# Computing the first norm's modulations as they land, and a shorter third mixer

## The chip, the cores and the metric

The program runs on one core of a Trainium2 chip. A core has TensorE (matrix products, here PE), VectorE (DVE), ScalarE (ACT), GpSimd (POOL) and SyncE (SP, which here only issues the loads and stores). The metric is the device time of one execution in microseconds, lower is better. Before the change it is 1545.95 us, the median of three runs (1545.14 to 1545.99).

## The reference

The reference runs three transformer-like layers on 256 tokens of width 1024: two layers of a "first block" and one of a "second block". What touches the change:

```python
def adaln_in(x, g, m, i):                   # norm, then scale and shift made from c
    return rmsnorm(x, g) * (1 + m[:, i, 1][:, None]) + m[:, i, 0][:, None]

cond = jax.nn.silu(c)
for l in range(DEPTH):                      # first block, 2 layers
    m = (cond @ w_mod[l] + b_mod[l]).reshape(bsz, 3, 3, D_MODEL)
    x = x + 0.5 * m[:, 0, 2] * swiglu(adaln_in(x, norm_g[l, 0], m, 0), w1, w3, w2)
    ...                                     # mixer, then a second swiglu
# second block, the third mixer's latent attention (8 heads of 64 + 32)
c_q = rms_norm(proj[..., OFF_CQ:OFF_CKV], q_a_norm)
c_kv = rms_norm(proj[..., OFF_CKV:OFF_KR], kv_a_norm)
q = (c_q @ w_uq).reshape(B_, S_, MLA_HEADS, QK_HEAD)
kv = (c_kv @ w_ukv).reshape(B_, S_, MLA_HEADS, QK_NOPE + V_DIM)
k = jnp.concatenate([k_nope, k_rope_h], axis=-1)   # one rotated part for all heads
q, k = rms_norm(q, q_norm), rms_norm(k, k_norm)    # then the rotary turn of the last 32
```

The very first thing that any layer needs is the shift `m[:, 0, 0]` and the scale `m[:, 0, 1]` of layer 0: 2048 numbers, each a product of `cond` (1024 values) with a column of `w_mod`.

## The kernel before, in words

Activations lie transposed: a chunk is 128 features by 256 tokens, and 8 chunks make the width of 1024. All large products are done in three passes of reduced-precision fp32 (`fp32r`): each weight unit of 128 x 1024 is split by ACT into a high part `WH` (line 1163) and by DVE into a low part `WL` (line 1662), and the activations likewise into `XH`, `XL` (or `GH`, `GL`). PE then sums WH*XH, WH*XL and WL*XH. The feed-forward parts run over 22 hidden chunks c: `up(c)` makes gate and value of chunk c (lines 642, 643, 646), `down(c-1)` adds the chunk before into eight output chunks in PSUM banks 0 to 3 (lines 697, 699, 704). A `low` pass is the one with WL.

The weights come through one SP queue in the order of a list, `stream_plan`, into a ring of three slots; SP waits where a slot is not yet read, and everything behind it in the list waits too. The modulation weights come through the same list, as items of three rows (`mod`, 1.5 MB) into scratch regions; a row is one DVE instruction pair (`mod_row`, line 1719), a 128 x 1024 product with `cond` summed along the free axis. In the prologue six items (18 rows, `HEAD_MODS`) come ahead of all feed-forward weights, DVE reduces them, and only then makes the gain (`adav`), the scaled chunks (line 1698) and their low parts (line 1710). ACT adds the shift (line 1208). The first unit's products, `first_up` (lines 658 and 664), take the chunks as they come.

In the third mixer (`win2_and_attention`) the twelve projection units of `win2` (line 781) are interleaved by hand with the latent attention's own products, which are in plain fp32: `q_pair` (lines 1002, and 1004 for the 32 swapped columns that the rotary turn needs), `lru_products` (line 1068), `k_pair` (lines 1015, and 1016, which copies the rotated key part `kr` through PE), `values` (1022), the sums of squares `cq_stats` (1031) and `q_stats` (1038), `k_sums` (1047, 1048) and `k_spread` (1058). A plain fp32 product is two passes in the trace. ACT's `gates` (line 1473) start when the low part of the memory's norm is done (`norm_low`, "mem", line 1708 on DVE); DVE also turns the queries (`q_rope`, lines 2160, 2161, 2167) and runs the short convolutions (`lru_convs`, line 2148). `take(b, ...)` makes PE wait for the last reader of bank b.

At the end of the last feed-forward part, the low pass of chunk 20 (line 681) is interleaved with the twenty-first's three passes (line 686).

Of the kernel before, what the change touches and what calls it, by code (L numbers as in the profile page):

```python
# [26 lines left out]
HEAD_MODS = 6  # L27
# [12 lines left out]
def columns(spec):  # L40
# [14 lines left out]
    ("eps", 1), ("inv", 1), ("halfpi", 1)])  # L55
# [9 lines left out]
def mod_plan():  # L65


    slot = {i: i for i in range(HEAD_MODS)}
    slot.update({i: i % 4 for i in range(HEAD_MODS, 20)})
# [4 lines left out]
    for f, (a, b, late) in enumerate([(HEAD_MODS, 20, 1), (22, 34, 1), (34, 46, 0), (46, 48, 2)]):  # L74
        n = b - a
        ffns[f] = {(k * (NFF - 1)) // n: a + k for k in range(n)}
        for c, i in ffns[f].items():
            for r in range(MOD_ROWS):
                h = 2 * c + late + r
                rows.setdefault((f, h // 2, h % 2), []).append((i, r))  # L80
# [10 lines left out]
def stream_plan():  # L91
# [3 lines left out]
    items = [(("mod", i), ITEM) for i in range(HEAD_MODS)]  # L95
# [42 lines left out]
WEIGHTS = [name for name, _ in ITEMS if name[0] not in ("mod", "lru")]  # L138
# [50 lines left out]
def build(nc, stream, param_d, const_d, bias_d, filter_d, x_d, mem_d, pos_d, c_d, out_d, known):  # L189
# [44 lines left out]
    def halves(name):  # L234
# [4 lines left out]
                 ring[:, (RING - 1) * ITEM:RING * ITEM]]  # L239
    rel = scr[:, ITEM:2 * ITEM].rearrange("p (h m) -> p h m", m=384)  # L240
# [31 lines left out]
    def landed(name):  # L272
# [3 lines left out]
        if name[0] == "mod":  # L276
            k = MOD_SLOT[name[1]]
            return sig.sem(f"mod_landed{k}"), 16 * sum(MOD_SLOT[i] == k for i in range(name[1] + 1))
# [45 lines left out]
    in_done = {8 * (3 * l + i) + 5: (l, i) for l in range(2) for i in range(3)}  # L324
# [202 lines left out]
    with nc.Block() as block:  # L527
# [3 lines left out]
        def _(sp):  # L531
            sp.dma_start(par[:, :], param_d).then_inc(*mark("par_in", n=16))
            sp.dma_start(cond[:, :], c_d.partition_broadcast(P)).then_inc(*mark("c_in", n=16))
            sp.dma_start(con[:, 0:2 * P], const_d[:, 0:2 * P]).then_inc(*mark("ones_in", n=16))
            for name, n in ITEMS:
                if name[0] == "mod":
                    i = name[1]
                    k = MOD_SLOT[i]
                    for p in [p for p in range(i) if MOD_SLOT[p] == k][-1:]:
                        sp.wait_ge(*at("mod_read", p))  # L540
# [11 lines left out]
                else:  # L552
                    i = PLACE[name]
                    if i == RING - 1:
                        sp.wait_ge(*at("mod_read", HEAD_MODS - 1))
# [7 lines left out]
                if name == ("mod", 1):  # L563
                    sp.dma_start(X, x_d).then_inc(*mark("x_in", n=16))
                if name == ("ffn", 0, 2):
                    sp.wait_ge(*at("mod_read", 4))
# [24 lines left out]
        def _(pe):  # L591
# [37 lines left out]
            def ffn(f):  # L629
# [19 lines left out]
                def first_up(b):  # L649

                    units = list(enumerate(up_units(f, 0)))
                    for k in range(KD):
                        pe.wait_ge(*at("norm_high", key, k))
                        for a, u in units:
                            for which, w in ((WH, ("high", u)), (WL, low_of(u))):
                                if k == 0:
                                    pe.wait_ge(*at(*w))
                                pe.matmul(b[:, a * S:(a + 1) * S], part(which, u, k), XH[:, k, :],  # L658
                                          start=(which is WH and a == 0 and k == 0), stop=False, skip_group_check=True)
                    for a, u in units:  # L660
# [5 lines left out]
                        last.then_inc(*mark("w1_used" if a == 0 else "ffn_up", f, 0))  # L666

                def down(c):
# [6 lines left out]

                    if c == NFF - 1:
# [23 lines left out]
                    if c == NFF - 2:  # L700
                        return
# [278 lines left out]
            uq = m[:, 0:1536].rearrange("p (k h n) -> p k h n", k=2, h=8)  # L980
            uq_swapped = m[:, 1536:2048].rearrange("p (k h n) -> p k h n", k=2, h=8)
# [11 lines left out]
            def q_pair(p):  # L993
                take(4 + p % 2, "q_turned", p)
                take(6 + p % 2, "q_turned", p)
# [3 lines left out]
                for i in range(2):  # L999
                    cols = slice(i * S, (i + 1) * S)  # L1000
                    for k in range(2):
                        pe.matmul(bank[4 + p % 2][0:96, cols], uq[:, k, 2 * p + i, :], PR[:, 8 + k, body], start=(k == 0), stop=(k == 1))
                    for k in range(2):
                        last = pe.matmul(bank[6 + p % 2][64:96, cols], uq_swapped[:, k, 2 * p + i, :], PR[:, 8 + k, body],
                                         start=(k == 0), stop=(k == 1))
                last.then_inc(*mark("q_product", p))

            def k_pair(p):
                take(4 + p % 2, "k_copied", p)
                if p == 0:  # L1010
                    pe.wait_ge(*at("normed", "ckv", 0))
                    pe.wait_ge(*at("kr_turned"))
                for i in range(2):
                    cols = slice(i * S, (i + 1) * S)
                    pe.matmul(bank[4 + p % 2][0:64, cols], uk[:, 2 * p + i, :], lat[:, 2, :], start=True, stop=True)
# [3 lines left out]
            def values():  # L1019
                for t in range(2):  # L1020
                    take(6 + t, "v_copied", t)
                    pe.matmul(bank[6 + t], lat[:, 2, t * P:(t + 1) * P], uv, start=True, stop=True)\
                        .then_inc(*mark("v_product", t))
# [9 lines left out]
            def q_stats():  # L1033

                pe.wait_ge(*at("q_squared", 3))
                for t in range(2):
                    for h in range(8):
                        last = pe.matmul(bank[6][:, 8 * t + h:8 * t + h + 1], SQ[0:96, h, t * P:(t + 1) * P], ones[0:96, 0:1],
                                         start=True, stop=True)
                last.then_inc(*mark("q_stat"))  # L1040
# [45 lines left out]
            def win2_and_attention():  # L1086
# [20 lines left out]
                cq_stats()  # L1107
                k_sums()
                q_stats()
# [42 lines left out]
        def _(act):  # L1152
# [295 lines left out]
            act.wait_ge(*at("c_in"))  # L1448
            act.activation(cond[:, :], cond[:, :], ACT.Silu).then_inc(*mark("cond"))
            for l in range(2):  # L1450
                if l == 0:
                    norm(("sub", 0, 0), lambda c: [("x_in",)], ahead=up_units(0, 0)[1])
# [1004 lines left out]
```

## Time and profile before

| | |
|---|---|
| median of three runs | 1545.95 us |
| the profiled execution | 1537.43 us |
| its span, first to last instruction | 1535.3 us |
| around the span | 2.1 us |
| PE busy | 1439.9 us, 94% |
| DVE busy | 1124.1 us, 73% |
| ACT busy | 705.1 us, 46% |
| DMA traffic | 309.29 MB |

Busy shares are means over the whole span, so the first 50 us and single stretches of the third mixer must be read by themselves. "Idle before" is the time an engine stood still ahead of an instruction, with the one that ended it. The granted clock is that of TensorE: 1.00 is 2.4 GHz, 0.50 is 1.2 GHz.

### The profile page before, as it was taken

What the parts mean: (1) busy time and instruction counts of PE and PEld (TensorE: products, weight loads), DVE (VectorE), ACT (ScalarE), POOL (GpSimd) and SP (SyncE); (2) the same over time, 40 slices, a digit from 0 to 9 for tenths busy, and PEclk for the clock granted to TensorE, in tenths of its full rate; (3) what the DMA queues carried; (4) which work ended last, traced back from release to release, by engine and by line L of the source; (5) the groups of instructions that cost most, each with busy time, mean ns of one, the idle gap of its engine ahead of it and who ended that gap; (6) DMA issues with size and microseconds to landing.
All of it is one profiled execution on the core that took longest, in us unless ns stands there. A gap on an engine that the chain in (4) does not pass through costs nothing.

```text
span 1535.3 us, 26554 instructions
## 1 busy us (share of the span) xinstructions
PE 1439.9 (94%) x10992; PEld 1349.6 (88%) x10992; DVE 1124.1 (73%) x1849; ACT 705.1 (46%) x1126; POOL 19.3 (1%) x16
## 2 busy tenths in 40 slices
PE   1999999999999989999999999999999879899998
PEld 1999998788999989999898689999976759799998
DVE  6888988867777788887667766565692766677776
ACT  2434445444343453334445344343544855554543
POOL 0000000000000000010000000000000120000000
PEclk8999999999999999999999999999999979999999
DMA  9986865156777548657333146654312203344541
GB/s 391 415 351 249 339 244 221 55 202 249 283 296 283 224 199 329 283 210 325 143 137 111 34 162 231 230 210 179 130 77 96 110 15 136 125 165 176 196 175 73
DMA packets 32327, 309.29 MB, mean 201 GB/s; under 512 B 3496, under 2 KB 5800, under 8 KB 7504
## 3 DMA queue, kind: packets, MB, share of 16 engines
q1 hardware_dynamic: 32208, 307.60, 52.0%
q8 instruction: 87, 1.43, 0.4%
q14 instruction: 32, 0.26, 0.0%
HBM read 306.53 MB, written 1.06 MB: 200 GB/s over the span
## 4 chain that ended last, share of the span: by engine, by line
PE 83%; DVE 10%; issue 3%; ACT 2%; DMA 2%; SPq 0%; DVEq 0%; ACTq 0%
PE bank L642 13%; PE bank L646 13%; PE bank L643 13%; PE bank L781 12%; PE bank L697 6%; PE bank L699 6%; PE bank L704 6%; DVE WL L1662 2%; PE bank L612 2%; PE bank L658 2%; DMA PR<-in_stream 1%; PE bank L861 1%; PE bank L686 1%; PE bank L850 1%; DVE tmp L1680 1%
## 5 line engine op out<-in xcount | busy, mean ns | idle before, releaser
L1662 DVE TENSOR_TENSOR WL<-ring,WH 128x1024 fp32r<-128x1024 f32 x420 | 504.1, 1226 | 51.3 <-ACT WH L1163 49.1
L1163 ACT ACTIVATE WH<-ring 128x1024 fp32r<-128x1024 f32 x420 | 429.6, 1053 | 135.2 <-PE bank L781 52.6
L642 PE MATMUL bank<-XH,WH 128*128 128x256 f32 x1680 | 410.1, 283 | 1.4 <-ACT WH L1163 1.4
L643 PE MATMUL bank<-XL,WH 128*128 128x256 f32 x1680 | 407.8, 281 | 0.0
L642 PEld LDWEIGHTS bank<-XH,WH 128*128 128x128 f32 x1680 | 316.2, 188 | 7.6 <-issue 6.0
L643 PEld LDWEIGHTS bank<-XL,WH 128*128 128x128 f32 x1680 | 316.2, 188 | 1.0 <-issue 1.0
L646 PE MATMUL bank<-XH,WL 128*128 128x256 f32 x1680 | 233.8, 282 | 1.0 <-DVE WL L1662 1.0
L646 PEld LDWEIGHTS bank<-XH,WL 128*128 128x128 f32 x1680 | 214.0, 188 | 1.2 <-DVE WL L1662 1.2
L1237 ACT ACTIVATE SG<-bank 128x256 f32<-128x256 f32 x88 | 33.8, 384 | 377.0 <-PE bank L646 363.5
L697 PE MATMUL bank<-GH,WH 128*128 128x256 f32 x840 | 202.6, 279 | 0.7 <-ACT WH L1163 0.7
L699 PE MATMUL bank<-GL,WH 128*128 128x256 f32 x840 | 202.5, 279 | 0.0
L697 PEld LDWEIGHTS bank<-GH,WH 128*128 128x128 f32 x840 | 157.5, 188 | 0.9 <-ACT WH L1163 0.9
L699 PEld LDWEIGHTS bank<-GL,WH 128*128 128x128 f32 x840 | 157.6, 188 | 0.0
L1784 DVE TENSOR_TENSOR tmp<-SG,bank 128x256 f32<-128x256 f32 x88 | 37.0, 421 | 154.6 <-ACT SG L1237 147.4
L704 PE MATMUL bank<-GH,WL 128*128 128x256 f32 x800 | 110.3, 279 | 0.0
L704 PEld LDWEIGHTS bank<-GH,WL 128*128 128x128 f32 x800 | 101.2, 188 | 0.0
L781 PE MATMUL bank<-XH,WH 128*128 128x256 f32 x512 | 90.4, 302 | 10.6 <-ACT XH L1208 7.1
L781 PEld LDWEIGHTS bank<-XH,WH 128*128 128x128 f32 x512 | 75.3, 199 | 21.6 <-issue 17.9
L781 PE MATMUL bank<-XH,WL 128*128 128x256 f32 x512 | 82.5, 285 | 0.0
L1771 DVE SCALAR_TENSOR_TENSOR scr<-bank,par,scr 128x255 f32<-128x255 f32 x88 | 38.4, 478 | 49.0 <-ACT scr L1230 48.2
L781 PE MATMUL bank<-XL,WH 128*128 128x256 f32 x512 | 74.1, 288 | 0.0
L781 PEld LDWEIGHTS bank<-XH,WL 128*128 128x128 f32 x512 | 72.4, 192 | 0.0
(306 smaller groups left out, 1698.8 us busy)
## 6 DMA issues: line engine op xcount, KB each, us to landing
ring<-in_stream SPq DMA_DIRECT2D x133, 1536.0 KB, 6.6
scr<-in_stream SPq DMA_DIRECT2D x15, 1536.0 KB, 10.8
PR<-in_stream SPq DMA_DIRECT2D x15, 1536.0 KB, 8.3
att<-in_stream SPq DMA_DIRECT2D x15, 1536.0 KB, 10.1
ring<-in_stream SPq DMA_DIRECT2D x8, 1024.0 KB, 5.0
ring<-in_stream SPq DMA_DIRECT2D x11, 512.0 KB, 3.6
kf_mix<-in_stream SPq DMA_DIRECT2D x2, 1536.0 KB, 16.0
con<-in_consts SPq DMA_DIRECT2D x1, 2000.0 KB, 19.7
```

The source lines that it names most:

```text
L642: pe.matmul(o, part(WH, u, k), XH[:, k, :], start=(k == 0), stop=False)
L643: pe.matmul(o, part(WH, u, k), XL[:, k, :], start=False, stop=False)
L646: last = pe.matmul(o, part(WL, u, k), XH[:, k, :], start=False, stop=(k == KD - 1))
L697: pe.matmul(out(m), part(WH, u, m), GH[:, c % 2, :], start=(c == 0 and m % 2 == 0), stop=False, skip_group_check=True)
L699: pe.matmul(out(m), part(WH, u, m), GL[:, c % 2, :], start=False, stop=False, skip_group_check=True)
L704: last = pe.matmul(out(m), part(WL, u, m), GH[:, c % 2, :], start=False, stop=False, skip_group_check=True)
L781: last = pe.matmul(o, lhs, rhs, start=first, stop=(p == parts[-1] and k == kc - 1), skip_group_check=True)
L1163: act.activation(part_all(WH, u), raw(u), ACT.Copy).then_inc(*mark("high", u))
L1237: act.activation(SG[:, c % 2, :], guc[:, c % 2, 0, :] if f == 4 else bank[4 + c % 2][:, 0:S], ACT.Silu)\
L1662: dve.tensor_tensor(part_all(WL, u), raw(u), part_all(WH, u).bitcast(F32), ALU.subtract)\
L1771: ins = dve.scalar_tensor_tensor(o, src, prm("fconv_w", 2 * NFF * k + col), o, ALU.mult, ALU.add)
L1784: dve.tensor_tensor(G32, SG[:, c % 2, :], second, ALU.mult).then_inc(*mark("g32", f, c))
```

## The change

There are three parts.

First, the prologue. The first 16 of the modulation's columns of layer 0 (8 of shift, 8 of scale) come as eight `head` items of 1 MB, one for each chunk: the scale's row for DVE and the shift's 1024 x 128 weights for PE. DVE reduces eight scale rows instead of 18 rows; PE makes each shift as eight plain fp32 products with one moving column (`cond_col`); ACT copies it out with its bias. Item 5 of the modulations (now the first `mod`) goes into a region that heads 1 and 2 use, so SP waits for both to be read. `first_up` has shifts and the low parts woven in for the first feed-forward.

Second, the last feed-forward's chunk 20 does its low pass itself, ahead of chunk 21.

Third, the mixer: the swapped query columns join the plain ones (96 + 32 = 128 columns in one product), the key's rotated part is copied by POOL instead of PE, `q_stats` goes pair by pair behind `k_pair`, `values` and `cq_stats` move.

```diff
-HEAD_MODS = 6
+HEAD_MODS = 5
     def ffn(f):
         for c in range(NFF + 1):
+            if (f, c) == (0, 0):
+                items.extend((("head", k), 2 * D) for k in range(3))
+            if (f, c) == (0, 1):
+                items.extend((("head", k), 2 * D) for k in range(3, KD))
...
+    head_before = {0: 1, 1: 2, 2: 4, 3: 5, 4: 7}
+                    if before:
+                        sp.wait_ge(*at("mod_read", before[-1]))
+                    else:
+                        sp.wait_ge(*at("scale_row", head_before[k]))
+                        sp.wait_ge(*at("shift_sum", head_before[k]))
...
                     for k in range(KD):
+                        if f == 0:
+                            for c in {0: range(4)}.get(k, range(k + 1, k + 2) if 3 <= k < 7 else ()):
+                                shift(c)
                         pe.wait_ge(*at("norm_high", key, k))
...
+                        if f == 0 and k >= 2:
+                            lows(k - 2)
...
+                def shift(c):
+                    pe.wait_ge(*at(f"head_landed{c}"))
...
+                    for k in range(KD):
+                        last = pe.matmul(bank[SHIFT_BANK[c]][:, c:c + 1], w[:, k, :], cond_col[:, k:k + 1], start=(k == 0), stop=(k == KD - 1),
+                                         skip_group_check=True)
+                    last.then_inc(*mark("shift_sum", c))
...
+                    if c == NFF - 1 and f == 4:
+                        pe.wait_ge(*at(*low_of(u)))
+                        for m in range(KD):
+                            for w, x in ((WH, GH), (WH, GL), (WL, GH)):
...
-                    for k in range(2):
-                        pe.matmul(bank[4 + p % 2][0:96, cols], uq[:, k, 2 * p + i, :], PR[:, 8 + k, body], start=(k == 0), stop=(k == 1))
-                    for k in range(2):
-                        last = pe.matmul(bank[6 + p % 2][64:96, cols], uq_swapped[:, k, 2 * p + i, :], PR[:, 8 + k, body],
-                                         start=(k == 0), stop=(k == 1))
+                    for k in range(2):
+                        last = pe.matmul(bank[4 + p % 2][:, cols], uq[:, k, 2 * p + i, :], PR[:, 8 + k, body], start=(k == 0),
+                                         stop=(k == 1))
...
-                    last = pe.matmul(bank[4 + p % 2][64:96, cols], ident[64:96, 64:96], kr, start=True, stop=True)
...
+                values(0)
+                cq_stats()
                 for p in range(4):
                     k_pair(p)
-                values()
+                    q_stats(p)
+                values(1)
...
+                    pool.wait_ge(*at("kr_turned"))
+                    for h in range(8):
+                        if h == 6:
+                            pool.wait_ge(*at("q_product", 3))
+                        ins = pool.tensor_copy(k96_pairs[h // 2][64:96, h % 2, :], kr)
...
+            for c in range(3):
+                scale_row(c)
+            norm_root(first)
+            for c in range(3):
+                head_scaled(c)
+            split_to(up_units(0, 0)[1])
+            for c in range(3, KD):
+                scale_row(c)
+                head_scaled(c)
+                norm_lows(first, range(c - 3, c - 2))
+            norm_lows(first, range(KD - 3, KD))
```

The SP queue at the program's start, before (the six `mod` items ahead of the first weights in `ring`):

```order
L534 DMA con<-in_consts 128x256
L548 DMA scr<-in_stream 128x3072 x2
L564 DMA X<-in_x 128x2048
L548 DMA PR<-in_stream 128x3072
L548 DMA att<-in_stream 128x3072
L548 DMA kf_mix<-in_stream 128x3072
L548 DMA ring<-in_stream 128x3072
L559 DMA ring<-in_stream 128x2048
L548 DMA PR<-in_stream 128x3072 [waits mod_read]
L559 DMA ring<-in_stream 128x3072
```

and after (128x2048 into `scr`, `PR`, `att` and `kf_mix` are heads 0 to 7):

```order
L544 DMA con<-in_consts 128x256
L545 DMA X<-in_x 128x2048
L548 DMA scr<-in_stream 128x2048 x3
L574 DMA ring<-in_stream 128x2048
L565 DMA scr<-in_stream 128x3072 [waits shift_sum,scale_row]
L548 DMA PR<-in_stream 128x2048 x2
L548 DMA att<-in_stream 128x2048
L548 DMA kf_mix<-in_stream 128x2048 x2
L574 DMA ring<-in_stream 128x3072
L565 DMA PR<-in_stream 128x3072 [waits shift_sum,scale_row]
```

Heads 3 to 7 now stand behind a wait for PE's and DVE's work on head 2.

PE from the norm's sums on, after (`knorm` holds `cond_col`; L708 is a shift's product, L684 the high and low-weight passes of `first_up`, L670 its low-activation passes). Before, nothing stands between the sums and the first `XH` products:

```order
L626 MATMUL bank<-SQ,con 128x256 [waits squared] x7
L708 MATMUL bank<-knorm,scr 128x1 [waits cond_col,head_landed0]
L708 MATMUL bank<-knorm,scr 128x1 x7
L708 MATMUL bank<-knorm,scr 128x1 [waits head_landed1]
L708 MATMUL bank<-knorm,scr 128x1 x7
L708 MATMUL bank<-knorm,scr 128x1 [waits head_landed2]
L708 MATMUL bank<-knorm,scr 128x1 x7
L708 MATMUL bank<-knorm,PR 128x1 [waits head_landed3]
L708 MATMUL bank<-knorm,PR 128x1 x7
L684 MATMUL bank<-XH,WH 128x256 [waits high,norm_high]
L684 MATMUL bank<-XH,WL 128x256 [waits low_dve]
```

Four shifts stand ahead of the first product with the norm's result, and one more is woven in ahead of each of chunks 3 to 6.

PE in the third mixer behind `lru_products`, before:

```order
L1015 MATMUL bank<-kf_mix,ring 64x256 [waits k_copied]
L1016 MATMUL bank<-tmp,con 32x256
L1015 MATMUL bank<-kf_mix,ring 64x256
L1016 MATMUL bank<-tmp,con 32x256
L1022 MATMUL bank<-ring,kf_mix 128x512 [waits q_turned] x2
```

and after (L1069 is `values`, L1077 `cq_stats`, L1062 `k_pair`, L1084 `q_stats`):

```order
L1069 MATMUL bank<-ring,kf_mix 128x512 [waits normed,kr_turned]
L1077 MATMUL bank<-con,kf_mix 128x1 [waits cq_squared,stat_root]
L1077 MATMUL bank<-con,kf_mix 128x1 x3
L1062 MATMUL bank<-kf_mix,ring 64x256 [waits normed,q_turned]
L1062 MATMUL bank<-kf_mix,ring 64x256
L1084 MATMUL bank<-con,SQ 128x1 [waits q_squared]
L1084 MATMUL bank<-con,SQ 128x1 x3
```

The copies through PE are gone, and the one-column sums of the queries stand between the key products.

## Rows read from the trace of the kernel before

**Rows 1.** The page's chain that ended last, share of the span by engine.
```profile
PE 83%; DVE 10%; issue 3%; ACT 2%; DMA 2%; SPq 0%; DVEq 0%; ACTq 0%
```
**Rows 2.** Timeline of 0 to 50 us: start, duration (us), engine, line, operation, idle before.
```profile
10.88 1.28 DVE L1719 CUSTOM_DVE_ANT_0 scr<-scr,cond,par 128x1024 f32<-128x1024 f32 x1 [10.88 <-DMA scr<-in_stream]
16.82 2.56 ACT L1187 ACTIVATE SQ<-X 128x256 f32<-128x256 f32 x8 [8.29 <-DMA X<-in_x]
17.38 5.48 PE L612 MATMUL bank<-SQ,con 128*128 128x256 f32 x16 [17.38 <-ACT SQ L1187]
...
33.97 2.00 ACT L1163 ACTIVATE WH<-ring 128x1024 fp32r<-128x1024 f32 x2 [10.53 <-DMA ring<-in_stream]
40.29 0.58 PE L658 MATMUL bank<-XH,WH 128*128 128x256 f32 x1 [17.42 <-ACT XH L1208]
46.24 2.06 PE L664 MATMUL bank<-XL,WH 128*128 128x256 f32 x16
49.72 0.39 PE L642 MATMUL bank<-XH,WH 128*128 128x256 f32 x1 [1.42 <-ACT WH L1163]
```
**Rows 3.** The page's DMA issues: form, count, KB each, us from issue to landing.
```profile
ring<-in_stream SPq DMA_DIRECT2D x133, 1536.0 KB, 6.6
ring<-in_stream SPq DMA_DIRECT2D x8, 1024.0 KB, 5.0
```
**Rows 4.** Stretches of the prologue: busy us (instructions) by engine, granted clock, DMA share, GB/s.
```profile
28.00:29.00 1.00, 0.00 (x0) 0.00 (x0) 1.00 (x3) 0.00 (x0) 0.00 (x0) 0.50 0.95 406
45.00:46.00 1.00, 1.00 (x10) 1.00 (x10) 0.63 (x2) 0.00 (x0) 0.00 (x0) 1.00 0.98 418
```
**Rows 5.** PE's groups by line, 1120 to 1195 us: busy us, mean ns.
```profile
L1004 PE MATMUL bank<-PR,ring 128*32 128x256 f32 x32 | 8.4, 384 | 0.0
```
**Rows 6.** Stretches of half a microsecond around the one-column sums, same columns as rows 4.
```profile
1181.00:1181.50 0.50, 0.50 (x6) 0.50 (x7) 0.50 (x1) 0.00 (x0) 0.00 (x0) 1.00 1.03 442
1182.00:1182.50 0.50, 0.50 (x4) 0.50 (x3) 0.24 (x1) 0.00 (x0) 0.00 (x0) 0.50 0.93 393
1188.50:1189.00 0.50, 0.50 (x6) 0.50 (x6) 0.00 (x0) 0.00 (x0) 0.00 (x0) 1.00 0.00 0
```
**Rows 7.** The chain that ended last, 1155 to 1194 us: start, us, what.
```profile
1155.34 0.48 ACT scr L1473
1155.86 5.45 PE bank L1068 x24
...
1169.15 0.57 PE bank L1015 x2
1169.72 0.55 PE bank L1016 x2
...
1179.89 5.38 PE bank L1038 x32
1185.27 4.40 PE bank L781 x24
```
**Rows 8.** Stretches of the mixer, same columns as rows 4.
```profile
1127.00:1140.00 13.00, 12.55 (x70) 8.05 (x69) 12.70 (x22) 6.06 (x12) 0.00 (x0) 1.00 0.01 2
1140.00:1152.40 12.40, 12.40 (x71) 8.02 (x70) 11.91 (x28) 1.37 (x3) 0.00 (x0) 1.00 0.00 0
```
**Rows 9.** POOL's and DVE's timelines near 1223 us.
```profile
1223.63 2.46 POOL L1631 TENSOR_TENSOR scr<-scr 128x1024 f32<-128x1024 f32 x1 [536.81 <-ACT scr L1562]
1243.39 0.72 POOL L1637 TENSOR_TENSOR PR<-PR,scr 128x256 f32<-128x256 f32 x1
...
1223.79 3.38 DVE L1662 TENSOR_TENSOR WL<-ring,WH 128x1024 fp32r<-128x1024 f32 x1
```
**Rows 10.** Timeline of the program's end, PE.
```profile
1526.49 0.55 PE L681 MATMUL bank<-GH,WL 128*128 128x256 f32 x1 [2.47 <-issue]
1529.62 0.33 PE L686 MATMUL bank<-GL,WH 128*128 128x256 f32 x1
1531.67 0.28 PE L686 MATMUL bank<-GH,WL 128*128 128x256 f32 x1
```

More of the change, by code:

```diff
@@ L65, in mod_plan @@
 def mod_plan():
-    slot = {i: i for i in range(HEAD_MODS)}
-    slot.update({i: i % 4 for i in range(HEAD_MODS, 20)})
+    slot = {i: i % 4 for i in range(HEAD_MODS, 20)}
     slot.update({20: 0, 21: 4})
@@ L91, in stream_plan @@
 def stream_plan():
-    items = [(("mod", i), ITEM) for i in range(HEAD_MODS)]
+    items = []
     units = []
@@ L137 @@
 ITEMS, UNITS = stream_plan()
-WEIGHTS = [name for name, _ in ITEMS if name[0] not in ("mod", "lru")]
+WEIGHTS = [name for name, _ in ITEMS if name[0] not in ("head", "mod", "lru")]
 PLACE = {name: i for i, name in enumerate(WEIGHTS)}
@@ L277, in landed @@
             k = MOD_SLOT[name[1]]
-            return sig.sem(f"mod_landed{k}"), 16 * sum(MOD_SLOT[i] == k for i in range(name[1] + 1))
+            return sig.sem(f"mod_landed{k}"), 16 * sum(MOD_SLOT[i] == k for i in range(HEAD_MODS, name[1] + 1))
         i = PLACE[name]
@@ L674, in out @@
                         return bank[m // 2][:, (m % 2) * S:(m % 2 + 1) * S]
+                    if c == NFF - 1 and f == 4:
+                        pe.wait_ge(*at(*low_of(u)))
+                        for m in range(KD):
+                            for w, x in ((WH, GH), (WH, GL), (WL, GH)):
+                                last = pe.matmul(out(m), part(w, u, m), x[:, c % 2, :], start=False, stop=(w is WL),
+                                                 skip_group_check=True)
+                            last.then_inc(*mark("ffn_out", f, m))
+                        return
                     if c == NFF - 1:
@@ L1448, in _, with shift, high @@
             act.wait_ge(*at("c_in"))
+            act.activation(cond_col[:, :], prm("c_col", 0, KD), ACT.Silu).then_inc(*mark("cond_col"))
             act.activation(cond[:, :], cond[:, :], ACT.Silu).then_inc(*mark("cond"))
+            def shift(c):
+                act.wait_ge(*at("shift_sum", c))
+                act.activation(modv[:, c:c + 1], bank[SHIFT_BANK[c]][:, c:c + 1], ACT.Identity, bias=prm("b_mod", c)).then_inc(*mark("shift", c))
+            def high(c):
+                act.wait_ge(*at("shift", c))
+                act.wait_ge(*at("scaled", ("sub", 0, 0), c))
+                act.activation(XH[:, c, :], norm_sq(("sub", 0, 0), c), ACT.Identity, bias=modv[:, c:c + 1])\
+                    .then_inc(*mark("norm_high", ("sub", 0, 0), c))
             for l in range(2):
                 if l == 0:
-                    norm(("sub", 0, 0), lambda c: [("x_in",)], ahead=up_units(0, 0)[1])
+                    squares(("sub", 0, 0), lambda c: [("x_in",)])
+                    load_table(ACT.Sqrt)
+                    root(("sub", 0, 0))
+                    for c in range(4):
+                        shift(c)
+                        if c == 2:
+                            split_to(up_units(0, 0)[1])
+                    for c in range(KD):
+                        if c >= 4:
+                            shift(c)
+                        high(c)
                 else:
@@ L2389, in lay_out @@
             blocks["mod", MOD_ITEMS * l + k] = m[k]
+    w = f["w_mod"][0]
+    shift = w[:, :D].reshape(KD, P, KD, P).transpose(2, 1, 0, 3)
+    scale = w[:, D:2 * D].T.reshape(KD, P, D)
+    for k in range(KD):
+        blocks["head", k] = np.concatenate([scale[k], shift[k].reshape(P, D)], 1)
     def ffn(n, w1, w3, w2):
```

123 lines of the change are left out of this document (74 added, 49 removed).

## Prediction

> **What bounds the kernel now.** The chain that ended last comes first: 83% of the span is PE [rows 1], so what takes PE's time, or makes it wait, is what counts. Three places are changed, and each must be read by itself, because the mean over the span says nothing of them.
>
> The prologue: the timeline shows PE idle for 17.42 us before its first product of the norm at 40.29, and the first unit ends at 48.30 (46.24 + 2.06); the second starts at 49.72 [rows 2]. Ahead of that stands DVE with its 18 rows of modulation, from 10.88 on [rows 2]. The loads keep the DMA engines full (share 0.95 to 0.98) [rows 4], so bytes count too. Two landings give their rate: the first item (2.4 MB with all ahead of it) is there at 10.88, the first weights (11.9 MB) at 33.97 [rows 2], which makes 2.43 us for each MB.
>
> The mixer: the chain runs over ACT's first gate at 1155.34, then without a gap over PE [rows 7]. But in the 25 us ahead of it DVE is busy for 12.70 of 13.00 and 11.91 of 12.40 us [rows 8]: both engines are full there.
>
> The end: PE stands still for 2.47 us before 1526.49, then has 32 products of which the last starts at 1531.67 [rows 10].
>
> **Prologue, step by step.** DVE loses ten rows ahead of the first unit; PE gains 8 shifts of 8 products of one column, each two passes: 128 passes. Their form is that of the one-column sums: 32 passes in 5.38 us [rows 7], of which about 1.86 us at the granted clock 1.00 (6 to 7 begun or running in each half microsecond) and 3.52 us at 0.50 (4) [rows 6]. This is 0.12 us each at 2.4 GHz (15.5 of them) and 0.21 at 1.2 GHz (16.5): 1.9 or 3.4 us for a shift.
>
> Which clock? PE was busy 0.50 of 0.50 us with these sums when the clock fell to 0.50, and it came back at 1188.5, about 3.3 us after the 256-column products had begun at 1185.27 [rows 6, 7]. The Trainium skill (TensorE: Matmul & The Clock Gate, What's actually happening) says that the gate is set by how busy PE has been recently. Read by the busy share, this would keep the clock up through the shifts; the row disagrees, since PE was fully busy and fell. I take the row: one-column passes don't hold the clock. What the other reading makes is the first rival.
>
> The times. x is now behind only 0.9 MB: 9.7 us (10.88 less 0.5 MB). Squares and sums take 6.0 us (16.82 to 22.86) [rows 2]: 15.7. Shifts 0 to 2 then need 5.7 us at 2.4 GHz, 10.2 at 1.2; I take 7.3, the clock falling on the way: 23. SP waits for shift 2 before it issues modulation item 5 (1.5 MB) and heads 3 to 7; the 5.9 MB ahead of them had landed by 19.4, so DMA stands empty. A load alone takes 5.0 us for 1 MB and 6.6 for 1.5 [rows 3], so about 2 us are fixed; head 3 lands at 23 + 2.1 + 2.5 x 2.43 = 31.2, head 7 at 40.9.
>
> PE has been idle for 8 us then, longer than the 5.1 us after which the clock was 0.50 in before (22.86 to 28) [rows 2, 4]. Shift 3 at 1.2 GHz ends at 34.6; ACT's copy and first high part take 0.7 (35.3). A 256-column pass costs 0.21 to 0.22 at this clock (14 from 1526.49 to 1529.62) [rows 10] and 0.12 at 2.4 GHz [rows 2]. Chunks 0 to 2 and the low part of 0 are 14 passes, 3.0 us: 38.3. Then four times a shift, four high and two low passes, 3.4 + 1.3 = 4.7 us: 57.0. Ten passes close it: 59.1. The 3.0 us of wide products should bring the clock back once, for some 3 us in which twice the work is done: 56. Before it was 48.3: +7.7. ACT's silu and split behind it stay (1.42 us [rows 2]); the second unit may start at 1.2 GHz where before it was at 1.00 [rows 4], +0.3. Sum +8.0. Bounds: +13.8 if all of it, shifts 0 to 2 too, is at 1.2 GHz (26.0, 34.2, 62.1), -3.8 if nothing is (shift 2 at 21.5, head 3 at 29.7, end 44.5). DVE needs 2.4 us for each late chunk and is hidden behind PE's 4.7; if PE took 2.6, it would be the two side by side. Two more rows of modulation fall to DVE inside the first feed-forward, where PE waited for DVE nowhere: 0.
>
> **Mixer, step by step.** Removed on PE: 32 passes of swapped columns. They show as 8.4 us busy in the row, overlapped; at 0.245 each they are 7.8 us of wall time [rows 5]. But DVE is as full as PE in that stretch [rows 8], and nothing is taken from DVE; ACT's gates wait for DVE's last low part of the memory's norm, at 1155.34 [rows 7]. So these 7.8 us bring 0: PE will wait for DVE's turned queries and ahead of the gates instead. It then waits for over 5 us, and starts the 24 passes of line 1068 at 1.2 GHz, +1.7 (half of some 3.4 us).
>
> From there PE is the chain. The key copies go, 8 times 0.55 [rows 7]: -4.4. The 32 one-column passes now stand in pairs between key products, at 0.12: 3.8 instead of 5.38, -1.6; unit 11 behind them took 4.40 for 24 passes, 2.84 at full clock, -1.6. `k_spread` needs the root of `k_sums`, 0.5 on ACT and 1.7 on DVE; unit 11 covers it with 2.84. Sum -5.9 with +1.7 in it.
>
> Added on POOL: eight copies of 32 x 256, beside DVE's full stretch. No such copy is in the trace; the nearest is a two-input operation of 128 x 256, 0.72 us undisturbed [rows 9]. When POOL's 2.46 us operation began at 1223.63, DVE's split, begun at 1223.79, took 3.38 us in place of some 1.2: it stood until POOL was done [rows 9]. Bounds: 0 and 8 x 0.72 = 5.8; some fall beside DVE's reciprocal or its PSUM readers, so I take 2.3. Mixer: -3.6, between -7.6 (no cold start, no lock) and -0.1 (both, the lock at 5.8). The Trainium skill (SBUF — State Buffer, Who interferes with whom) calls the port pair of the two an exclusive lock, where the second fully blocks if DVE reads two SBUF operands. DVE's convolutions and splits do; by it the sum would be nearer to the upper bound, which is the second rival.
>
> **End.** Eight of the 32 passes move into the 2.47 us of waiting. The other 24 take 2.8 us at 2.4 GHz instead of 5.35 (-2.5), or 4.3 if the clock still falls (15 at 0.21) (-1.1) [rows 10]. The idle time shrinks to 1.5 us; I take -2.2.
>
> **Sum.** +8.0 - 3.6 - 2.2 = +2.2. The profiled execution took 1537.43 us, 1535.3 of span and 2.1 around it: 1539.6. It was 8.5 us (0.55%) below the median of the runs shown, 1545.95; the difference is carried over as it is: 1548.2 us. About 0.2%, 3.1 us, is what a measurement of this kernel can tell from no change.
>
> **Rivals.**
> 1. The one-column passes do hold or restore the clock. For: before 17.38 PE had been idle, and nothing in the page says what counts; against: rows 6. Then shifts 0 to 2 end at 21.5, head 3 lands at 29.7, shift 3 is still slow (33.1), and all behind it fast: 14 x 0.12 = 1.7, four times 2.6, 1.2: 47.2 with ACT's 0.7, -1.1. Total -1.1 - 3.6 - 2.2 = -6.9: 1539.0. Chance 0.16.
> 2. POOL's lock: slower. Each of the eight copies holds DVE's two-operand work for its full 0.72 us; +5.8 in place of 2.3 makes the mixer -0.1, the total +5.7: 1551.7. For: rows 9; against: 32 partitions and one input may be shorter. From a DVE delay of 3.2 us on, the sum is over the 3.1 us. Chance 0.15.
> 3. The clock stays at 1.2 GHz through the whole of the first unit, without the one recovery: 59.1, or up to 62.1. +11 to +14 in place of 8: about 1552 to 1554. Chance 0.12.
> 4. PE is the bound in the mixer after all, and DVE follows: -7.8 - 4.4 - 3.2 = -15.4; total -9.6: 1536.3. Against: rows 8. Chance 0.06.
> The forecast has 0.51, with a range of its own of 1545 to 1551.
>
> **Chances.** Faster than by 0.2%: rival 1, rival 4 and 0.03 of the forecast's case, 0.25. Slower: rivals 2 and 3 and a fifth of the forecast's case, 0.37. Within: 0.38. The range leaves out rival 4 and the far end of 3: 1538.5 to 1554.
>
> **What would show it.** Right: SP's issue of the `mod` item behind the first weights waits for PE until 21 to 25 us; DMA has an empty stretch near 20 to 25; the clock is 0.50 through most of 31 to 56, with the shifts' passes at 0.21 us; the second unit begins at 56 to 60. In the mixer PE idles ahead of the third `q_pair` and over 5 us ahead of the gates, which begin at the same distance from the stretch's start as before or later; POOL's copies stand beside lengthened DVE operations; 8 passes fill the wait at the end. Wrong: the second unit begins before 50 us, or the gates begin over 3 us earlier.

## The result, and the profile after

| | before | after |
|---|---|---|
| median of 20 runs each | 1545.97 us (1540.26 to 1550.83) | 1553.75 us (1541.32 to 1557.39) |
| ratio | | 1.0046, 95% interval 1.0029 to 1.0062 |
| profiled execution, span | 1537.43, 1535.3 us | 1554.27, 1552.5 us |
| mean granted clock | 0.979 | 0.963 |

The change makes the kernel some 7 us slower. The median is inside the forecast's range by 0.25 us, and not where the forecast put it: the prologue loses more than was said, and that is nearly all of the difference.

**Prologue.** The timeline after (start, duration, engine, line, operation, idle before), to set beside [rows 2]; L708 is a shift's product, L656 the second unit:

```profile
9.59 6.50 PE L626 MATMUL bank<-SQ,con 128*128 128x256 f32 x16 [9.59 <-ACT SQ L1235]
15.93 7.71 PE L708 MATMUL bank<-knorm,scr 128*128 128x1 f32 x48
...
23.73 0.33 SPq L565 DMA_DIRECT2D scr<-in_stream  x1
...
32.59 3.57 PE L708 MATMUL bank<-knorm,PR 128*128 128x1 f32 x16 [8.96 <-DMA PR<-in_stream]
40.07 3.41 PE L708 MATMUL bank<-knorm,PR 128*128 128x1 f32 x16
44.76 3.41 PE L708 MATMUL bank<-knorm,att 128*128 128x1 f32 x16
...
62.69 0.55 PE L656 MATMUL bank<-XH,WH 128*128 128x256 f32 x1 [1.51 <-ACT WH L1211]
```

Stretches of it (busy us by engine in the order PE, PEld, DVE, ACT, POOL, then granted clock, DMA share, GB/s), to set beside [rows 4]:

```profile
16.00:17.00 1.00, 1.00 (x12) 1.00 (x10) 0.67 (x1) 0.47 (x1) 0.00 (x0) 1.00 1.04 442
18.00:19.00 1.00, 1.00 (x9) 1.00 (x10) 1.00 (x1) 0.07 (x1) 0.00 (x0) 0.85 0.02 8
22.00:23.00 1.00, 1.00 (x6) 1.00 (x6) 0.00 (x0) 0.00 (x0) 0.00 (x0) 0.50 0.00 0
50.00:51.00 1.00, 1.00 (x6) 1.00 (x6) 0.00 (x0) 0.00 (x0) 0.00 (x0) 0.50 0.92 393
60.00:61.00 1.00, 1.00 (x6) 0.88 (x5) 0.00 (x0) 0.00 (x0) 0.00 (x0) 0.50 1.07 455
66.00:67.00 1.00, 1.00 (x9) 1.00 (x8) 1.00 (x2) 0.00 (x0) 0.00 (x0) 0.76 0.93 400
```

SP issues the waiting item at 23.73, 0.1 us after the last product of shift 2, and DMA moves next to nothing at 18 and nothing at 22 us. PE then has nothing for 8.96 us. The clock falls to 1.2 GHz near 19 us, while PE is busy 1.00 of 1.00 us with one-column passes, and is back only in the microsecond that begins at 66. The second unit starts 13.0 us later than at 49.72 [rows 2].

**Mixer.** PE's timeline after (L1052 `q_pair`, L1115 the gates' products, L1062 `k_pair`, L1084 `q_stats`, L902 the first scores), to set beside [rows 7]:

```profile
1163.21 3.78 PE L1052 MATMUL bank<-PR,ring 128*128 128x256 f32 x8 [4.36 <-DVE kf_mix L2257]
...
1178.42 7.13 PE L1115 MATMUL bank<-scr,att 128*128 128x256 f32 x24 [4.20 <-ACT scr L1543]
...
1187.13 1.08 PE L1062 MATMUL bank<-kf_mix,ring 128*64 128x256 f32 x4
1188.14 1.05 PE L1084 MATMUL bank<-con,SQ 96*128 96x1 f32 x8
...
1209.66 2.68 PE L902 MATMUL bank<-PR,kf_mix 96*128 96x256 f32 x6
```

The 7.8 us that the merge takes from PE are idle time now: 4.36 us ahead of the third pair, and 4.20 us ahead of the gates' products where 1.51 us stood before. Behind the gates, key products and sums in pairs take about 1.0 us each.

POOL's copies and DVE at the same time (`WL` is a split with two SBUF inputs, `kf_mix` a scaling):

```profile
1150.18 3.16 POOL L1703 COPY PR<-tmp 32x256 f32<-32x256 f32 x6 [444.37 <-DVE tmp L2235]
1172.56 0.74 POOL L1703 COPY PR<-tmp 32x256 f32<-32x256 f32 x2 [19.21 <-PE bank L1052]
...
1150.15 1.22 DVE L1740 TENSOR_TENSOR WL<-ring,WH 128x1024 fp32r<-128x1024 f32 x1
1153.07 0.55 DVE L1776 SCALAR_TENSOR_TENSOR kf_mix<-PR,par,tmp 128x256 f32<-128x256 f32 x1
```

and the same scaling before:

```profile
1130.62 0.48 DVE L1698 SCALAR_TENSOR_TENSOR kf_mix<-PR,par,tmp 128x256 f32<-128x256 f32 x1
```

DVE's split takes 1.22 us, the page's mean for this line (1225 ns). The scaling began under the sixth copy and took 0.07 us longer than before; no other DVE operation there is lengthened. The eight copies by themselves (least, median and longest, ns):

```profile
L1703 POOL COPY PR<-tmp x8: 393/395/1448, 1150.2 to 1172.9; 32x256 f32<-32x256 f32 x8
```

**End.** PE's timeline, to set beside [rows 10]:

```profile
1542.69 1.12 PE L756 MATMUL bank<-GH,WL 128*128 128x256 f32 x8
1545.26 0.36 PE L724 MATMUL bank<-GH,WH 128*128 128x256 f32 x1 [1.46 <-issue]
1548.09 0.28 PE L724 MATMUL bank<-GH,WL 128*128 128x256 f32 x1
```

From the first to the last start are 2.83 us for 24 passes, where it was 5.18 for 32.

### The profile page after: what moved, and what is told of

The parts are those of the page before. It is cut to its first block, busy times and chain, and to the rows that moved or that the text cites. A ratio compares the mean times of both kernels' runs of the same rounds, so it can differ in the third digit from the quotient of the medians.

```text
span 1552.5 us, 26743 instructions
## 1 busy us (share of the span) xinstructions
PE 1466.1 (94%) x11072; PEld 1385.9 (89%) x11072; DVE 1116.7 (72%) x1840; ACT 707.6 (46%) x1135; POOL 23.2 (1%) x24
## 4 chain that ended last, share of the span: by engine, by line
PE 85%; DVE 9%; issue 3%; ACT 2%; DMA 1%; SPq 0%; DVEq 0%; ACTq 0%
PE bank L656 13%; PE bank L660 13%; PE bank L657 13%; PE bank L833 12%; PE bank L749 6%; PE bank L751 6%; PE bank L756 6%; PE bank L626 2%; PE bank L684 2%; DVE WL L1740 2%; PE bank L708 2%; PE bank L913 1%; PE bank L902 1%; PE bank L738 1%; DVE tmp L1758 1%
## 5 line engine op out<-in xcount | busy, mean ns | idle before, releaser
L1740 DVE TENSOR_TENSOR WL<-ring,WH 128x1024 fp32r<-128x1024 f32 x420 | 503.9, 1225 | 54.4 <-ACT WH L1211 50.4
L656 PE MATMUL bank<-XH,WH 128*128 128x256 f32 x1680 | 411.0, 283 | 1.5 <-ACT WH L1211 1.5
L656 PEld LDWEIGHTS bank<-XH,WH 128*128 128x128 f32 x1680 | 317.8, 189 | 7.8 <-issue 7.8
L749 PE MATMUL bank<-GH,WH 128*128 128x256 f32 x840 | 206.2, 284 | 0.8 <-ACT WH L1211 0.8
L751 PE MATMUL bank<-GL,WH 128*128 128x256 f32 x840 | 206.2, 281 | 0.0
L1849 DVE SCALAR_TENSOR_TENSOR scr<-bank,par,scr 128x255 f32<-128x255 f32 x88 | 38.5, 478 | 50.1 <-ACT scr L1278 49.3
```

Source lines behind the costliest of these rows:

```text
L656: pe.matmul(o, part(WH, u, k), XH[:, k, :], start=(k == 0), stop=False)
L749: pe.matmul(out(m), part(WH, u, m), GH[:, c % 2, :], start=(c == 0 and m % 2 == 0), stop=False, skip_group_check=True)
L751: pe.matmul(out(m), part(WH, u, m), GL[:, c % 2, :], start=False, stop=False, skip_group_check=True)
L1740: dve.tensor_tensor(part_all(WL, u), raw(u), part_all(WH, u).bitcast(F32), ALU.subtract)\
L1849: ins = dve.scalar_tensor_tensor(o, src, prm("fconv_w", 2 * NFF * k + col), o, ALU.mult, ALU.add)
```

## The experiments

The ratios are to runs of the kernel before on the same chip; its medians beside e1 to e4, e5 to e8 and e9 to e12 were 1544.21, 1542.66 and 1543.13 us.

**The parts apart.** e1 has the diff's hunks of the prologue, e2 those of the mixer and the end.

> Only the first part of the change (heads, shifts on PE, scale rows on DVE), the mixer and the end as before. Theory A (the loss is made in the prologue, by a late second unit): the second unit starts 10 to 14 us later than in the kernel before and the whole is 9 to 16 us slower, ratio 1.006 to 1.010. Rival B (the whole change's loss is mostly falls of the granted clock at other places, which one profile of each shows by chance): the prologue alone costs under 5 us. Forecast on record: +8.0.

> The mixer's and the end's parts alone, the prologue as before. Theory A: 6 to 8 us faster (mixer -4 to -6, end -2.3), ratio 0.995 to 0.996. Rival B (the mixer brings nothing, since a cold start of the scores behind it and of the gates' products takes the gain): -2 to -3, ratio 0.998 to 0.999. POOL's eight copies beside DVE: by the rows of the changed kernel 0, by the lock of the prediction +2 to +6, which would show as gates' products that begin later against the stretch's start.

Measured: e1 1558.7 us, ratio 1.0092 (1.0061 to 1.0123), +14.2 us. e2 1538.3 us, 0.9958 (0.9936 to 0.998), -6.5 us. The sum, +7.7, is close to the whole change's +7.1. All of the loss is in the prologue; rival B of e1 falls (the lower end of e1's interval is +9.4 us), and the -2 to -3 us of e2's rival lie just outside e2's interval (-3.1 to -9.9).

**The queue and the width.** e3 lets no load wait for shift 2:

```diff
 def ffn(f):                                # stream_plan
-            if (f, c) == (0, 1):
-                items.extend((("head", k), 2 * D) for k in range(3, KD))
...
             items.append((("ffn", f, c), UNIT * len(names)))
+            if (f, c) == (0, 0):
+                items.extend((("head", k), 2 * D) for k in range(3, KD))
             if c in MODS_OF.get(f, {}):
```

> As the first, with one edit: heads 3 to 7 stand in the load queue ahead of the modulation item that waits for shift 2, so no load waits for PE. Theory A: head 3 lands at 21 instead of 32.6 us, PE goes from shift 2 to shift 3 without a gap, first unit ends near 52 instead of 61, whole 8 to 10 us faster than the first kernel (ratio to before 1.000 to 1.003). Rival C (the eight shifts at 1.2 GHz are what takes the time, the empty queue is covered): the first unit ends at 57 or later, under 4 us faster than the first.

The first unit then ends at 50.1 us, which excludes rival C's 57 or later.

e9 changes only the width of a shift's moving operand, e5 both:

```diff
-    cond_col = knorm
+    cond_col = sb("cond_wide", P + 8)       # silu of 136 columns, the last 8 are c's
...
-   pe.matmul(bank[SHIFT_BANK[c]][:, c:c + 1], w[:, k, :], cond_col[:, k:k + 1], ...
+   pe.matmul(bank[SHIFT_BANK[c]][:, 0:P], w[:, k, :], cond_col[:, k + 1:k + 1 + P], ...
```

> As e3_order, and the moving operand of a shift's products is 128 columns wide instead of one (the 128th column is the wanted one, the others are read and left in PSUM). Theory A (one-column passes let the clock fall and don't bring it back, wide ones hold it): granted clock 1.00 from 15 us on, a shift in 1.9 to 2.2 instead of 3.4 us, chunk period 2.6 instead of 4.7, first unit ends at 38 to 41 instead of 50.1, ratio to before 0.995 to 0.998. Rival E (the clock falls because of something else that these products share, their plain fp32 form or the small gaps between them): clock 0.50 from about 20 us on, and the wider passes make it slower than e3_order, ratio 1.003 or over.

> As e1_prologue, with only the 128 column wide moving operand; heads 3 to 7 still behind the item that waits. Theory A (two causes, the queue's wait and the clock, that can be taken away one by one): shifts 0 to 2 end at 20 to 21 instead of 23.8, head 3 lands 2.5 to 3.5 us earlier, at 29 to 30; PE has been idle for 9 us and the clock is 0.50 when it starts again, but the wide passes bring it back some 5 us later; the second unit starts at 49 to 54 instead of 62.6; ratio to before 0.999 to 1.004, between e1 and e5. If the clock were the only cause: as e5, 0.996.

| | one column | 128 columns |
|---|---|---|
| heads 3 to 7 behind the wait | e1: 1.0092, +14.2 us, unit 2 at 62.55 | e9: 1.0037 (1.0022 to 1.0052), +5.7 us, unit 2 at 50.90 |
| ahead of it | e3: 1.0027 (1.0008 to 1.0045), +4.2 us, unit 2 at 51.61 | e5: 0.9961 (0.9939 to 0.9983), -6.0 us, unit 2 at 41.39 |

The timeline of e3:

```profile
21.52 3.57 PE L708 MATMUL bank<-knorm,PR 128*128 128x1 f32 x16 [0.89 <-DMA PR<-in_stream]
28.99 3.41 PE L708 MATMUL bank<-knorm,PR 128*128 128x1 f32 x16
...
51.61 0.36 PE L656 MATMUL bank<-XH,WH 128*128 128x256 f32 x1 [1.51 <-ACT WH L1207]
```

PE's idle time ahead of shift 3 is 0.89 instead of 8.96 us. And of e5:

```profile
29.06 1.95 PE L708 MATMUL bank<-cond_wide,att 128*128 128x128 f32 x16
31.56 1.95 PE L708 MATMUL bank<-cond_wide,kf_mix 128*128 128x128 f32 x16
...
37.48 0.87 PE L670 MATMUL bank<-XL,WH 128*128 128x256 f32 x6
...
41.39 0.55 PE L656 MATMUL bank<-XH,WH 128*128 128x256 f32 x1 [3.04 <-ACT WH L1207]
```

A shift of 128 columns takes 1.95 us, one of a single column 3.41. The same microsecond in e3 and in e5:

```profile
30.00:31.00 1.00, 1.00 (x7) 1.00 (x6) 0.93 (x5) 0.00 (x0) 0.00 (x0) 0.50 1.06 442
```

```profile
30.00:31.00 1.00, 1.00 (x11) 1.00 (x11) 1.00 (x3) 0.00 (x0) 0.00 (x0) 1.00 1.10 459
```

PE is busy 1.00 us in both; one is at 1.2 GHz, the other at 2.4. Only the moving operand's width differs between the two kernels, so the width is the cause. Theory A's numbers for the first unit came in (its end: 38.4), and so did the ratio. The clock did not stay up for good: it fell in PE's idle time of 3.04 us ahead of the second unit and read 0.50 from 40 to 46 us. Rival E (the plain fp32 form or the gaps) falls. The Trainium skill (TensorE: Matmul & The Clock Gate, What's actually happening) says that the gate is set by how busy the PE has been recently. By the busy time that the profile shows, this would have kept e3 at full clock; the measurement decides, and the sentence holds here only if "busy" means something else than that share.

In e9 the queue's wait stands:

```profile
29.67 3.78 PE L708 MATMUL bank<-cond_wide,PR 128*128 128x128 f32 x16 [8.74 <-DMA PR<-in_stream]
...
37.35 2.19 PE L708 MATMUL bank<-cond_wide,PR 128*128 128x128 f32 x16
40.10 1.95 PE L708 MATMUL bank<-cond_wide,att 128*128 128x128 f32 x16
```

Shift 3 is slow behind 8.74 us of idle time, wide or not (3.78); the clock is back in the microsecond from 37, about 8 us after PE had started again, where some 5 were expected. In e1, with one column, it is back only in the microsecond from 65. Head 3 lands at 29.7 and the second unit starts at 50.90, both as expected. So the order alone is worth 10.0 us, the width alone 8.5, both 20.2. By the intervals each of these differences is known to some 5 us; by the start of unit 2 they are 10.9, 11.7 and 21.2. There are two causes, nearly additive.

**Another way to the same end.** e4 is e3 with the shifts of chunks 4 to 7 as rows on DVE:

```diff
+                if c >= PE_SHIFTS:          # 4
+                    s = head_slots[c][:, D:2 * D]
+                    dve.tensor_tensor_reduce(s, s, cond[:, :], 1.0, prm("b_mod", c), ALU.mult, ALU.add,
+                                             accum_out=modv[:, c:c + 1]).then_inc(*mark("shift", c))
```

> As the third, and shifts 4 to 7 are made by DVE as rows, like the scales (1.3 us each), and only 0 to 3 by PE. Theory A (3.4 us on PE for a shift of one-column passes at 1.2 GHz is the dear part once the queue is free): PE has shifts 0 to 3 behind it at 27, DVE ends its rows near 42, first unit ends at 43 to 46, second unit 3 to 6 us earlier than in the kernel before; ratio 0.996 to 0.999. Rival D (DVE becomes the bound, since it was full in the prologue of the kernel before): first unit ends at 48 or later, ratio 1.000 or over.

Measured: 1544.09 us, 1.0002 (0.998 to 1.0024). The first unit ends at 46.0, the late edge of what was expected; the second starts at 47.45, 2.3 us earlier than before instead of 3 to 6, and the runs don't tell that from nothing. DVE is the bound in it: PE waits for DVE's low parts four times, 1.04 to 2.43 us each.

```profile
36.30 0.79 PE L674 MATMUL bank<-XL,WH 128*128 128x256 f32 x2 [2.43 <-DVE XL L1783]
```

So rival D's mechanism takes most of the gain. e4 also shows when the clock comes back without one-column passes: behind shift 3 it has only wide ones, 18 of them from 27.65 to about 31.9 us, and the clock is at 1.00 in the microsecond from 33. It is at 0.50 again in that from 36, behind the wait of 2.43 us (columns as in the stretches above):

```profile
33.00:34.00 1.00, 0.87 (x6) 0.67 (x6) 1.00 (x3) 0.05 (x1) 0.00 (x0) 1.00 1.01 430
36.00:37.00 1.00, 0.70 (x3) 0.70 (x4) 1.00 (x2) 0.45 (x1) 0.00 (x0) 0.50 0.98 418
```

**The mixer's parts.** e7 is the kernel before with the merge of the query columns alone, e6 is e2 without it (the merge is the diff's lines of `q_pair`, with the matching ones of `q_rope`).

> The kernel before with only the merge of the swapped query columns into the plain ones. Theory A: PE's 7.8 us turn into idle time ahead of the third pair and of the gates, 0 to +2 us, ratio 1.000 to 1.001. Rival F: -4 to -8 us, ratio 0.995 to 0.997.

> As e2_mixer_tail, but the swapped query columns are products of their own again, as in the kernel before (32 more passes). Theory A (DVE sets the pace there, the merge only makes PE idle and lets its clock fall ahead of the gates): the gates' products begin at the same place against the stretch's start, take 5.5 instead of 7.1 us, whole 0 to 2 us faster than e2 (ratio to before 0.994 to 0.996). Rival F (PE is the bound, the merge is worth its passes): 4 to 8 us slower than e2, ratio 0.999 to 1.001.

Measured: e7 1547.18 us, 1.0014 (0.9992 to 1.0035); e6 1538.07 us, 0.9949 (0.9924 to 0.9974) beside e2's 0.9958. Neither shows a gain or a loss of the merge beyond its interval; rival F's 4 to 8 us are excluded. The place shows why. From the memory norm's last sums to the gates' products are 36.15 us before (1119.71 to 1155.86), 36.09 after (1142.33 to 1178.42), 35.78 in e7, 36.05 in e6, 35.71 in e2: PE's work between does not set it. e7:

```profile
1148.56 3.53 PE L1000 MATMUL bank<-PR,ring 128*128 128x256 f32 x8 [3.95 <-DVE kf_mix L2157]
...
1163.78 8.18 PE L1064 MATMUL bank<-scr,att 128*128 128x256 f32 x24 [5.25 <-ACT scr L1469]
```

What the merge takes from PE comes back as 3.95 and 5.25 us of idle time, and the gates' products take 8.18 instead of 5.45 us. In e6 they took 7.13 behind only 1.92 us of idle time, so the start at 1.2 GHz that e6 should have saved was there without the merge too; that half of my expectation missed. In the six other profiles without the merge (before, e1, e3, e4, e5, e9) the wait is 1.51 to 1.63 us and the products take 5.45. So the 1.7 us are not shown to be the merge's alone.

e12 is e2 with the key's rotated part copied by PE again:

```diff
-                    last = pe.matmul(bank[4 + p % 2][0:64, cols], uk[:, 2 * p + i, :], lat[:, 2, :], start=True, stop=True)
+                    pe.matmul(bank[4 + p % 2][0:64, cols], uk[:, 2 * p + i, :], lat[:, 2, :], start=True, stop=True)
+                    last = pe.matmul(bank[4 + p % 2][64:96, cols], ident[64:96, 64:96], kr, start=True, stop=True)
```

> As e2_mixer_tail, but the rotated key part is copied by PE again, eight products of 0.55 us between the key products, instead of by POOL. Theory A: scores begin 4 to 4.6 us later against the memory norm's sum than in e2 (66.9), at about 71.3; ratio to before 0.998 to 0.999. If POOL's copies had cost DVE something (the lock), the difference is smaller, down to 0.

Measured: 1548.22 us, 1.0038 (1.0018 to 1.0058), some 12 us over e2 by the ratios. I had expected 4 to 5: a miss, and by much. From the gates' products to the scores are 47.94 us (1157.12 to 1205.06) against 31.21 in e2. The timeline of e12 (L1019 key products, L1020 the copies, L1042 the sums):

```profile
1168.46 0.61 PE L1020 MATMUL bank<-tmp,con 32*32 32x256 f32 x2
1169.00 1.64 PE L1042 MATMUL bank<-con,SQ 96*128 96x1 f32 x8
1170.58 1.11 PE L1019 MATMUL bank<-kf_mix,ring 128*64 128x256 f32 x2
1171.62 1.06 PE L1020 MATMUL bank<-tmp,con 32*32 32x256 f32 x2
...
1186.36 1.87 PE L1042 MATMUL bank<-con,SQ 96*128 96x1 f32 x8
```

At 1169 the clock falls, and stays at 0.50 until the full-width products of unit 10; between, copies of 32 x 32 weights and one-column sums alternate, and each takes twice its time. In the kernel before, copies and key products alternate without such sums from 1161.24 to 1170.20, each copy at 0.55 us. The sums in pairs kept the clock up only without the copies, and not always then. The same stretch is 31.17 to 31.40 us long in four profiles of the new mixer (after, e2, e6, e10), and 34.42 and 34.46 in two (e8, e11), where the clock fell in it. In e11:

```profile
1166.00:1169.00 3.00, 3.00 (x18) 2.17 (x18) 0.00 (x0) 2.60 (x6) 0.00 (x0) 0.92 0.00 0
1169.00:1172.00 3.00, 3.00 (x12) 2.14 (x11) 0.00 (x0) 1.57 (x4) 0.00 (x0) 0.50 0.00 0
```

With the old mixer it was 37.36 in the profile of before and 38.92 to 39.25 in five others (e1, e3, e4, e5, e9), so the typical gain here is 1.6 us larger than before's own profile says. At the end it is the other way round: the old end's 32 passes took 5.18 us in before's profile and 5.11 in e7's, where the clock was at 0.50 for some of them, but 3.78 or 3.79 in those five, at full clock (in e3 from 1540.23 to 1544.02). Against 2.83 that is 1.0 us instead of 2.35.

**Put together.** e8 is the changed kernel with e4's prologue, e10 with e5's two edits, e11 moves one item more:

```diff
-            if c in MODS_OF.get(f, {}):
+            if (f, c) == (0, 1):
+                items.append((("mod", MODS_OF[0][0]), ITEM))
+            if c in MODS_OF.get(f, {}) and (f, c) != (0, 0):
                 items.append((("mod", MODS_OF[f][c]), ITEM))
```

> The changed kernel with e4_half's prologue (heads 3 to 7 ahead of the waiting item, shifts 4 to 7 on DVE). Theory A (the parts add up): before + e4 (0) + e2 (-6.5): ratio 0.995 to 0.997, and 13 to 15 us under the changed kernel. If the parts don't add (the clock's falls move and eat the gain): 0.998 or over.

> The changed kernel with e5's two edits (heads 3 to 7 ahead of the waiting item, moving operand of 128 columns). If the parts add up: e5 (-4.5 to -6) and e2 (-6.5): 11 to 13 us under before, ratio 0.991 to 0.993.

> As e10, and the first modulation item of 1.5 MB stands behind the second unit's weights instead of ahead of them. Theory: in e5 PE stood idle 3.04 us ahead of the second unit for these weights and fell to 1.2 GHz there (41.4 to 47); now they land 3.6 us earlier, the wait is ACT's split alone (about 1.5), the clock stays at 1.00: second unit starts at 39.9, another 2 to 4 us less than e10, ratio 0.989 to 0.991. Rival: the wait was not the loads' but ACT's and DVE's; no change to e10.

Measured: e8 1537.65 us, 0.9965 (0.9942 to 0.9988); e10 1530.43 us, 0.9922 (0.9899 to 0.9944); e11 1529.71 us, 0.9914 (0.9893 to 0.9935). The parts add up within the intervals in all three; e8 is by the ratios 12.5 us under the changed kernel, where 13 to 15 were expected. e10 is 12.0 us under the kernel before, and by ratios (1.0046 against 0.9922) some 19 us under the changed kernel. The difference between e10 and e11 is not resolved, so the further 2 to 4 us are a miss, and their mechanism is not seen either: e10's second unit starts at 40.85, e11's at 40.99, both behind ACT's split.

```profile
40.85 0.36 PE L656 MATMUL bank<-XH,WH 128*128 128x256 f32 x1 [1.63 <-ACT WH L1211]
```

```profile
40.99 0.36 PE L658 MATMUL bank<-XH,WH 128*128 128x256 f32 x1 [1.51 <-ACT WH L1213]
```

PE's wait ahead of the second unit, 3.04 us in e5, is 1.63 in e10, so there was hardly anything for e11 to take. In e5 ACT had waited 1.42 us for these weights until 40.19; in e10 it began its split at 39.65 without a wait. Why e10's weights were there in time and e5's not stays open.

## Why the prediction was right in its range and wrong in its steps

- **The queue's wait: right.** Forecast: shift 2 done at 23, head 3 at 31.2. Measured 23.64 and 32.58, and DMA stood empty ahead of SP's issue at 23.73. e3 prices it at 10.0 us.
- **One-column passes don't hold the clock: right, and now shown.** Forecast 3.4 us for a shift at 1.2 GHz and 4.7 for a chunk's cycle; measured 3.41 and 4.70 (40.07 to 44.76). e5 takes the cause away, and the same passes of 128 columns ran at 2.4 GHz.
- **The one recovery of the clock: wrong, and this is the step that failed.** "The 3.0 us of wide products should bring the clock back once" was worth -3 us. It did not come: the 14 wide passes behind shift 3 took 3.2 us (36.91 to 40.07), all at 1.2 GHz, then shift 4 followed with its one-column passes, and all else up to 66 us was slow too. In e4, where only wide passes followed shift 3, the clock was still 0.50 in the microsecond from 31, and 1.00 in that from 33. The first unit ended at 61.2 against 56: 3.1 of the 5.2 us is the recovery that did not come (59.1 was the all-slow case), 1.4 is head 3's landing, the rest small. That was rival 3, which had 0.12 and gave 1552 to 1554.
- **The second unit's start: too small.** +0.3 for a start at 1.2 GHz; it ran so from 62.69 to about 66.2, 3.5 us, of which half is lost: 1.8. In e3, e9 and e10 the second unit began at full clock, in e5 and e8 not. Together the prologue was +8.0 in the forecast and +14.2 in e1.
- **The merge brings nothing: right.** Third pair and gates wait as said (4.20 us ahead of the gates' products, where over 5 were forecast), and the gates start at the same distance. Their products take 1.7 us more (7.13 against 5.45), as forecast, though e6 took as long without the merge. Rival 4 falls with e7.
- **Key copies and sums: right for this pair of profiles.** Copies and sums took 8.96 + 5.30 us of wall time before (1161.24 to 1170.20, 1179.83 to 1185.13) and take 7.89 after, with the keys' products in both (1187.13 to 1195.02): -6.4 against -6.0 forecast. Unit 11: 4.47 to 3.05, -1.4 against -1.6. That the clock held through the new order was luck as much as foresight: it fell there in e8 and e11 (3.2 us more), and in e12, with the copies left in, it cost some 12 us.
- **POOL's lock: wrong.** +2.3 was in the sum; the copies cost 0 on the path. The median copy took 0.39 us; the longest, the first, 1.45, while DVE's two-input split ran from 1150.15 to 1151.37. DVE began 0.03 us ahead of it, and what POOL lost was off the path. This is the other side of the rule cited in the prediction (the Trainium skill, SBUF — State Buffer, Who interferes with whom): the trace fits an exclusive hold in which the second one waits, and here the second was the one that nobody waits for. It doesn't prove the hold: that copy is also POOL's first behind 444 us of idle time, and no run separates the two. The next five ran almost wholly beside DVE's reciprocal, which reads one SBUF operand, and the only DVE operation that began under a copy lost 0.07 us. So the schedule kept the two apart; copies against two-input operations of DVE were hardly tested. Rival 2 falls for this kernel. Without the term the mixer's forecast would have been -5.9; measured -6.1 from gates to scores, and about -7.7 against the five other profiles of the old mixer.
- **The end: right for this pair of profiles, and in part luck.** 2.83 us for 24 passes instead of 5.18 for 32: -2.35 against -2.2. But 1.4 of it is the clock, which stood at 0.50 for some 14 of before's passes; against the five profiles where the old end ran at full clock (3.79 us) it is -1.0, and in e8 the new end itself was slow (4.32).

So +8.0 - 3.6 - 2.2 = +2.2 was the forecast's sum and +14.2 - 6.5 = +7.7 is the measured one. The prologue's loss was forecast 6.2 us too small. The gain elsewhere was 0.7 us too small by the medians (5.8 against 6.5), and 2.7 by the places in the two traces (6.1 and 2.35).

That the range holds the result is luck in good part. The forecast's own case, 1545 to 1551, was missed; the wide range reached to 1554 for rival 3's sake, and the median is 1553.75. Had the mixer and the end won only the 5.8 us of the forecast, the time would have been outside it.

## What to carry to other kernels

Read the granted clock, not the busy share, where TensorE works on narrow operands: one-column products showed it 100% busy while it ran at half speed, and padding the same products to 128 columns took a shift from 3.41 to 1.95 us and put all that is woven between the shifts at full clock. Before a list of loads gets an item that waits for compute, put ahead of it all that does not have to wait: here five heads stood behind one wait, which cost 10 us. And a merge that takes 8 us from a busy engine is worth nothing where another engine sets the date; look at the distance between two marks that the engine does not set.

## What the runs showed of the hardware beyond expectation

- A shift's 16 passes of 128 columns took 1.95 us and of one column 3.41; where both were at full clock they cost the same: 48 passes from 14.67 in 5.52 us (e5, wide) and from 14.95 in 5.68 us (e3, one column, the clock at 0.97 in the last full microsecond and 0.50 behind it).

```profile
14.67 5.52 PE L708 MATMUL bank<-cond_wide,scr 128*128 128x128 f32 x48
```

```profile
14.95 5.68 PE L708 MATMUL bank<-knorm,scr 128*128 128x1 f32 x48
```

- The clock falls at other places in each profile (gates to scores of one and the same mixer took 31.2 or 34.4 us by it), and this may well be much of the spread of one kernel: the changed kernel's fastest run of 20 (1541.32 us) has a mean granted clock of 0.973, its slowest (1557.39) of 0.961. A profile's total is therefore a poor measure of a change of 5 us. The distance between two marks is a better one, but it too needs the clock beside it and more than one profile: from gates to scores it moved by 3.2 us, and over the end's passes by 1.4, with no change to the kernel there.
- A copy of 32 x 256 values took POOL 0.39 us, about half of the 0.72 us of the nearest row before, a two-input operation of 128 x 256 [rows 9].
